# The feature-wise projections of a two-block language-model kernel: one 512-column matmul for the high weights, blocks of 256 features

## What is computed

```
zxbcdt = x @ w_in            # 2048 -> 10304: z, xs, B, C, dt
xbc = silu(conv4(xbc) + b);  y = chunked_scan(xs, dt, a, B, C) + xs * d
h = group_rms(y * silu(z)) * norm_w @ w_out;        x = layernorm(ALPHA * x + h)
k, v = x @ kv_w + kv_b;  q, gate = x @ w_bi         # window attention with sinks
x = layernorm(ALPHA * x + (attention(q, k, v) * silu(gate)) @ w_bo)
x = x + neighbourhood_attention(rms(x) @ w_qkv) @ w_o
x = x + relu(rms(x) @ w_1)**2 @ w_2                 # hidden size 8192
```

## Time and profile before

| | us |
|---|---|
| median of 3 runs | 2156.46 (2156.21 to 2156.93) |
| the profiled execution | 2156.41 |
| its span, first to last instruction | 2154.6 |
| PE busy in the span | 2138.8 (99%) |
| DVE busy | 1347.5 (63%) |
| ACT busy | 1124.4 (52%) |
| POOL busy | 18.4 |
| granted TensorE clock, mean | 1.000, so 2.4 GHz |

### The profile page before, as it was taken

The page is one execution under the profiler, slowest core; times in us unless marked ns, Lnnn a source line. Parts: engine busy times, 40 slices in busy tenths (PEclk is TensorE's granted clock), DMA queues, the critical chain, the costliest instruction groups (busy, mean ns, idle before and its releaser), DMA issues.

```text
span 2154.6 us, 33241 instructions
## 1 busy us (share of the span) xinstructions
PE 2138.8 (99%) x13589; PEld 1920.5 (89%) x13589; DVE 1347.5 (63%) x2126; ACT 1124.4 (52%) x1903; POOL 18.4 (1%) x30
## 2 busy tenths in 40 slices
PE   8999999999999999999999999999999999999999
PEld 8999999999887878998788888889998889999887
DVE  6877777777655887755855555555554445555443
ACT  5565666666444555643645666544444334444332
POOL 0000000000000000000000000000000000000000
PEclk9999999999999999999999999999999999999999
DMA  7555555555675543466565554455556665555664
GB/s 267 192 186 183 188 193 172 182 187 194 215 239 177 192 152 127 140 221 192 168 215 193 179 174 151 149 183 181 183 185 192 191 194 186 185 184 185 192 213 136
DMA packets 109640, 399.55 MB, mean 185 GB/s; under 512 B 12128, under 2 KB 12512, under 8 KB 108848
## 3 DMA queue, kind: packets, MB, share of 16 engines
q1 hardware_dynamic: 105552, 378.73, 54.4%
q0 software_dynamic: 3936, 18.70, 2.4%
HBM read 395.21 MB, written 2.16 MB: 184 GB/s over the span
## 4 chain that ended last, share of the span: by engine, by line
PE 97%; DVE 2%; ACT 1%; DMA 0%; issue 0%; SPq 0%; ACTq 0%; DVEq 0%
PE ps L1460 95%; PE ps L1463 2%; DVE wlo L862 1%; ACT lnt L556 0%; DMA raw<-in_w_in 0%; DVE xlo L862 0%; DVE small L868 0%; ACT xhi L559 0%; DVE res L871 0%; ACT whi L559 0%; DVE sms L865 0%; DVE sms L862 0%; DVE red L1270 0%; DVE qt L862 0%; DVE small L1120 0%
## 5 line engine op out<-in xcount | busy, mean ns | idle before, releaser
L862 DVE TENSOR_TENSOR wlo<-raw,whi 128x1024 fp32r<-128x1024 f32 (+1 forms) x713 | 869.9, 1223 | 664.5 <-ACT whi L559 662.9
L559 ACT ACTIVATE whi<-raw 128x1024 fp32r<-128x1024 f32 (+1 forms) x713 | 753.6, 1059 | 976.2 <-PE ps L1460 963.4
L1460 PE MATMUL ps<-xhi,whi 128*128 128x256 f32 x2560 | 728.7, 285 | 6.0 <-ACT whi L559 6.0
L1460 PE MATMUL ps<-xhi,wlo 128*128 128x256 f32 x2560 | 723.8, 283 | 0.7 <-DVE wlo L862 0.7
L1460 PE MATMUL ps<-xlo,whi 128*128 128x256 f32 x2560 | 723.7, 283 | 0.0
L1460 PEld LDWEIGHTS ps<-xhi,whi 128*128 128x128 f32 x2560 | 491.2, 192 | 10.4 <-issue 9.6
L1460 PEld LDWEIGHTS ps<-xhi,wlo 128*128 128x128 f32 x2560 | 491.1, 192 | 0.9 <-DVE wlo L862 0.9
L1460 PEld LDWEIGHTS ps<-xlo,whi 128*128 128x128 f32 x2560 | 491.3, 192 | 0.0
L1460 PE MATMUL ps<-whi,xhi 128*128 128x512 f32 x544 | 215.7, 402 | 3.1 <-ACT xhi L559 2.5
L1460 PE MATMUL ps<-whi,xlo 128*128 128x512 f32 x544 | 209.5, 392 | 0.1
L1460 PE MATMUL ps<-wlo,xhi 128*128 128x512 f32 x544 | 208.3, 390 | 0.0
(11 more groups left out here) (201 smaller groups left out, 1968.8 us busy)
## 6 DMA issues: line engine op xcount, KB each, us to landing
raw<-in_w SPq DMA_DIRECT2D x256, 512.0 KB, 3.5
raw<-in_w_in SPq DMA_DIRECT2D x159, 512.0 KB, 3.5
raw<-in_w_qkv SPq DMA_DIRECT2D x96, 512.0 KB, 3.5
raw<-in_w_ao SPq DMA_DIRECT2D x64, 512.0 KB, 4.3
raw<-in_w_bi SPq DMA_DIRECT2D x64, 512.0 KB, 3.5
raw<-in_w_bo SPq DMA_DIRECT2D x32, 512.0 KB, 4.4
raw<-in_w_o SPq DMA_DIRECT2D x32, 512.0 KB, 3.4
cum<-scratch POOLq DMA_DIRECT2D x8, 1024.0 KB, 5.9
```

The lines of the kernel that those rows point to most:

```text
L559: return eng.activation(out, x, ACT.Copy, **kw)
L862: return eng.tensor_tensor(out, x, y, op)
L1460: return eng.matmul(out, x, y, start=start, stop=stop, skip_group_check=True)
```

## The change

It has four parts, all in the feature-wise units.
- The two activation parts lie side by side (`xhl`: for each row 256 columns high, then 256 low). One matmul of 512 columns passes both through `whi` (called product 3), and one of 256 passes the high part through `wlo` (product 2). A block now fills a bank: columns 0 to 255 hold high x high, columns 256 to 511 the two others.
- So a unit is two blocks (256 features), and a slot four rows of 256 columns. There are 40 `in`, 8 `gate` and 32 `w1` units of four slots each. The number of slots, of visits and of bytes is unchanged.
- The halves are added at the end: ScalarE copies the second half of both banks to SBUF, VectorE adds the first half from PSUM onto it (`add_parts`). What follows (taps, tanh, silu, relu and square) reads the sum in SBUF. The banks come free when the sum is there, two visits after the unit's end at the earliest.
- The first two units of `in` and of each half of `w1` take turns slot by slot (`woven`), so that new rows of the activations are asked for as slowly as before.

```diff
-        self.tiles = nk // 2
+        self.rows = 4 if feat else 2
+        self.tiles = nk // self.rows
...
+    woven(features("in", 0, "w_in"), features("in", 1, "w_in"))
+    for n in range(2, 40):
+        slots.extend(features("in", n, "w_in"))
...
-            order = [(b, p) for p in range(3) for b in range(4)] if i == 0 else [(b, p) for b in range(4) for p in range(3)]
-            visits.append((i, None, [(i, 2 * j + h, b, p) for h in range(2) for b, p in order]))
+            order = [(b, p) for p in range(3) for b in range(2)] if i == 0 else [(b, p) for b in range(2) for p in (3, 2)]
+            visits.append((i, None, [(i, 4 * j + h, b, p) for h in range(4) for b, p in order]))
...
+            def copy_others(u, out):
+                w.wait_ge(S["weights"], END[u, 0])
+                w.wait_ge(S["weights"], END[u, 1])
+                return copy(out, main_and_rest(u)[1])
@@ in_proj on ScalarE @@
+                yield
+                w.wait_ge(S["conv"], convs_before[max(n - 1, 0)])
+                copy_others(INDEX["in", n], sums[:, n % 2, :, :]).then_inc(S["part"], 1)
+                yield 2
+                w.wait_ge(S["sum"], n + 1)
@@ in_proj on VectorE @@
+                yield 2
+                w.wait_ge(S["part"], n + 1)
+                add_parts(INDEX["in", n], sums[:, n % 2, :, :]).then_inc(S["sum"], 1)
                 yield 2
                 last = {}
                 for s in (1, 2, 3):
...
-                        i = stt(z[:, s:T], feature_bank(u, b)[:, 0:T - s], t[3 - s], ALU.mult, z[:, s:T], ALU.add)
+                        i = stt(z[:, s:T], sums[:, n % 2, b, 0:T - s], t[3 - s], ALU.mult, z[:, s:T], ALU.add)
...
-                    yield
-                yield
+                    if s == 1:
+                        yield
+                yield 2
@@ hidden on VectorE @@
+                add_parts(INDEX["w1", U], x.rearrange("p (k t) -> p k t", k=2)).then_inc(S["hsum"], 1)
+                w.wait_ge(S["hsum"], U + 1)
+                stt(x, x, 0.0, ALU.max, x, ALU.mult).then_inc(S["hsqr"], 1)
@@ wait_for_banks on TensorE @@
-                    w.wait_ge(S["tanh"], 4 * n + 4)
+                    w.wait_ge(S["sum"], n + 1)
...
+                    if p == 3:
+                        q = mul(bank, left, xhl[:, k, :, :].rearrange("p s t -> p (s t)"), start=k == 0, stop=False)
```

More of the change, by code:

```diff
@@ L72, in held_back, with woven, features @@
             slots.extend(part)
-    for n in range(20):
-        slots.extend(unit("in", n, "w_in", 8 * n, 16, feat=True))
+    def woven(a, b):
+        for pair in zip(a, b):
+            slots.extend(pair)
+    def features(stage, n, src):
+        return unit(stage, n, src, 4 * n, 16, feat=True)
+    woven(features("in", 0, "w_in"), features("in", 1, "w_in"))
+    for n in range(2, 40):
+        slots.extend(features("in", n, "w_in"))
     held_back(*[unit("ao", n, "w_ao", 16 * n, 32, apart="end" if n == 3 else None) for n in range(4)])
@@ L79, in plan @@
         slots.extend(unit("q", n, "w_bi", 8 * n, 16))
-    for n in range(4):
-        slots.extend(unit("gate", n, "w_bi", 32 + 8 * n, 16, feat=True))
+    for n in range(8):
+        slots.extend(features("gate", n, "w_gate"))
     held_back(*[unit("bo", n, "w_bo", 8 * n, 16, apart="end" if n == 3 else None) for n in range(4)])
@@ L89, in plan @@
     for half in range(2):
-        for n in range(8):
-            slots.extend(unit("w1", 8 * half + n, "w_1", 64 * half + 8 * n, 16, feat=True))
+        woven(features("w1", 16 * half, "w_1"), features("w1", 16 * half + 1, "w_1"))
+        for n in range(2, 16):
+            slots.extend(features("w1", 16 * half + n, "w_1"))
         held_back(*[unit("w2", 4 * half + n, "w_2", 64 * half + 16 * n, 32) for n in range(4)])
@@ L136, in marks @@
             last["used", i] = v, m
-            last["end", u, t // 2 if units[u].feat else t] = v, m
+            last["end", u, t] = v, m
     used, end, count, where = {}, {}, {}, {}
@@ L154, in feed @@
     sync, high, low = out[0]
-    for k in range(2):
-        for z in (sync, high, low):
-            z.extend([("x", k, 1), ("w", 0, k)])
+    for z in (sync, high, low):
+        z.extend([("x", 0, 1), ("w", 0, 0), ("x", 1, 1), ("x", 2, 2), ("w", 0, 1)])
     on = {"fetched": 1, "high": 1, "low": 1}
@@ L599, in in_proj @@
                     t, shift = taps(g, x)
-                    act(ACT.Identity, place(g, x), feature_bank(u, b), bias=shift, scale=t[3]).then_inc(S["ev"], 1)
-                yield 4
-                w.wait_ge(S["ssum"], sum(scan_at(g) + 18 < ended("in", n) + 5 for g in range(GROUPS)))
+                    act(ACT.Identity, place(g, x), sums[:, n % 2, b, :], bias=shift, scale=t[3]).then_inc(S["ev"], 1)
+                yield 3
                 for b, x in enumerate(blocks_of[n]):
-                    w.wait_ge(S["made"], 4 * (n - 1) + b + 1)
+                    w.wait_ge(S["made"], 2 * (n - 1) + b + 1)
                     if b in convs[n]:
@@ L713, in gates @@
             def gates(n):
-                u = INDEX["gate", n]
                 yield
                 w.wait_ge(S["roped"], 5)
[L717 to L727, removed]
+                w.wait_ge(S["g_low"], n - 1)
+                copy_others(INDEX["gate", n], gate[:, n % 2, 0, :].rearrange("p (k t) -> p k t", k=2)).then_inc(S["gpart"], 1)
+                yield 2
+                w.wait_ge(S["gsum"], n + 1)
+                act(ACT.Tanh, gate[:, n % 2, 1, :], gate[:, n % 2, 0, :], scale=0.5).then_inc(S["g_tanh"], 1)
+                yield 2
+                w.wait_ge(S["g_z"], n + 1)
+                copy(ghi[:, 2 * n:2 * n + 2, :], gate[:, n % 2, 0, :].rearrange("p (k t) -> p k t", k=2)).then_inc(S["g_high"], 1)
             def values(n):
@@ L1416, in vector_program @@
             side.at(19, rope_tables())
[L1417 removed]
+            for n in range(40):
                 side.at(ended("in", n), in_proj(n))
@@ L1531, in product @@
                 if unit.feat:
-                    right = factor(unit, k, (0, 1), p == 1)
-                    left = weight(i, k, p == 2)
-                    q = mul(feature_bank(u, x), left[:, x * P:x * P + P], right[:, k, :], start=k == 0 and x % 2 == 0 and p == 0, stop=last)
+                    left = weight(i, k, p == 2)[:, x * P:x * P + P]
+                    bank = ps[:, banks(u)[x], :]
+                    if p == 3:
+                        factor(unit, k, (0, 1), 0)
+                        factor(unit, k, (0, 1), 1)
+                        q = mul(bank, left, xhl[:, k, :, :].rearrange("p s t -> p (s t)"), start=k == 0, stop=False)
+                    else:
+                        right = factor(unit, k, (0, 1), p == 1)[:, k, :]
+                        q = mul(bank[:, 0:T] if p == 0 else bank[:, T:2 * T], left, right, start=k == 0 and p == 0, stop=last)
                 else:
```

157 lines of the change are left out of this document (75 added, 82 removed).

## The result

The changed kernel takes **2145.25 us** (median of 4 runs, 2144.99 to 2145.81) where the kernel before takes 2156.36 on the same chip: a ratio of 0.9948 with a 95% interval of [0.9931, 0.9966]. It is faster, by 11.1 us, but 8 us outside the range that was given and 16.7 us above the forecast.

A forecast was written before the change was run, and what follows sets the result against it. The prediction took PE's instruction stream to bound the kernel. From 2156.4 us it took 34.2 for the merge and added 5.3 (slot 16) and 1.1 (woven pairs): 2128.6 us, range 2122 to 2137.

The forecast's parts named there:

- What bounds the kernel: Whole kernel: PE's instruction stream sets the time, as long as the other engines stay ahead.
- The merge, -34.2 us: Feature-wise units: 2552 triples become a 512 and a 256, each saving 13.4 ns (360.0 to 346.6), all on the path.
- rival 3: Feature-wise units: the fixed part stays when widths alternate, a triple keeps 360.0 ns, 2162.8 us; chance 4%.
- Slot 16, +5.3 us: Near the start, PE waits for unit 2's addition, queued on DVE behind the time-step chain: +5.3 us.
- The woven pairs, +1.1 us: Units taking turns in `in` and each half of `w1`: PE waits 0.5 us and twice 0.3 us for additions.
- DVE and ACT at nothing: Steady stages: DVE's extra additions and ACT's extra copies hide behind PE's stream and cost nothing.
- Rivals 1 and 4: Small waits in many places, 2136 to 2143 us, 13%; the bank stall in every group, 2165.6 us, 5%.
- All but the merge: The stall at slot 16 and the waits of the woven pairs together: +6.4 us.

The follow-up runs named there:

- split: The changed kernel with the merge undone, so every matmul of the feature-wise groups has 256 columns: 2164.73 us, 1.0035 of the kernel before.
- add_first: The changed kernel with the in-projection steps, including the halves' addition, ahead of the time steps in DVE's side work: 2139.48 us, 0.9921 of the kernel before.
- kick: The changed kernel with order 512, 512, 256, 256 in the first 128 rows of each slot, alternating in the rest: 2139.24 us.
- lead_add: The changed kernel with the addition ahead of the time steps and runs of two in the first of each block's four slots: 2134.81 us.
- cross: The changed kernel, widths still alternating, but each 256 behind a 512 adds to the other bank than that 512: 2145.46 us.
- other_half: The changed kernel with the 256-column matmul adding to columns 0 to 255 of its bank instead of 256 to 511: 2145.28 us.

## Why the prediction was wrong

**What bounds the kernel**: right. PE 99% before and after, and the chain that ended last is 96% PE.

**The merge, -34.2 us**: this is the step that failed. It read: "I take 346.6, because the fixed part is equal at either width, so nothing in it seems to depend on the neighbour." That the fixed part is equal holds for uniform streams, before and after (120.0 ns in *split*, 226.6 in `w2`). The second half does not follow from it, and it is wrong: in strict alternation a triple took 353.3 ns in `w1` and in about two thirds of each `in` group, and 346.7 only in the rest (17% of all triples, counted by start times). *split* against the changed kernel puts the merge at 18.8 us, so the term was 15.4 us too large, most of the 16.7 us by which the forecast was too low. 353.3 lay within the bounds named in that step (320 to 360.0), but no rival stood for a part of the fixed cost: rival 3 kept all of it, with 4%, and the range left it out. Half of 34.2 lost would have given 2145.7. An unshown adjacency between two known rows should have kept its upper bound in the range.

The Trainium skill ("TensorE: Matmul & The Clock Gate", section "Back-to-back issue gap") gives N/2.4 + 2.5 ns for a matmul alone. For load and matmul pairs that is not what is seen here, neither uniform (120.0 ns for 256 columns in *split*, 226.6 for 512 in `w2`) nor mixed (353.3 or 346.7 for the two).

**Slot 16, +5.3 us**: the mechanism, the place and the wait were right (PE idle 5.21 us, from DVE's `sums` at 62.61 to 63.31 us; the forecast had it ready 16.4 us after PE went on with slot 12, and it was 63.31 - 46.89 = 16.4). Its price was not: the clock fell during the wait and slot 16 took 4.91 us, 2.1 more than at full clock. The prediction did not say a word on the clock. *add_first* supports the sum: it took away 5.21 + 2.1, put 0.63 of new waits in their place, and gained 5.8 us, 6.3 between the two traced executions, where this makes 6.7.

**The woven pairs, +1.1 us**: slot 8 waited 0.49 us for `sums` (0.5 forecast), and each half of `w1` has a wait of 0.24 (0.3 forecast). Place and idle time are right. By start times they cost more than they stand idle: from slot 7 to slot 9 are 6.37 us where two slots without a wait take 5.60, and each wait in `w1` costs 0.5 in the same way, so 1.8 in all.

```profile
PE ps L1476 <- DVE rl L878: 0.5, 2, 0.2
```

**DVE and ACT at nothing**: right. No wait of PE for either shows from 100 to 510 us. DVE's busy time rose to 1395.7 (near 1398 forecast), ACT's by 22.1 us (25 forecast). Rivals 1 and 4 did not occur.

**All but the merge** was forecast at +6.4 us. With the clock's 2.1 it is 8.5, and by start times 9.2 (7.4 at slot 16, 1.8 at the woven pairs). *split* measured 7.5 [4.7, 10.4].

**The sum again**: 2156.4 - 18.8 + 7.5 = 2145.1, measured 2145.25. The two parts are both taken from *split*, so this sum is no test of its own. The trace alone gives one: -17.0 (2552 x 6.67) - 3.0 (some 450 triples in the quick rhythm, 6.67 more each) + 7.4 (slot 16: from the last matmul of slot 15 at 57.87 to the one behind slot 16 at 68.20 are 10.33 us, where some 2.95 would do without stall and slow clock) + 1.8 (the three other waits) makes 2145.6. The traced execution took 2145.81.

**What stays open**: why TensorE loses 20 ns in three triples in one rhythm and nothing in the other, and what about an interruption selects it. That a turned row always switches the rhythm in *kick* is seen, not explained, and neither *lead_add* nor the waits follow so simple a rule. The runs exclude the bank, the half of the bank, the merged matmul by itself and a fixed price per change of width. The number of changes matters in no simple way (1 in 1: 0 or 6.7 ns a triple; runs of two 1.7; of four 3.3 to 4.2; of eight 2.5).

## What to carry to other kernels

A saving that rests on "so many matmuls fewer" is safe only for streams that the trace shows. Where two widths are going to stand side by side for the first time, keep the full fixed cost as an end of the range, and try several orders of the same matmuls: here a one-line change of order was worth almost as much as the whole edit (9.5 against 11.1 us). When an edit makes TensorE wait on a vector engine's side work, first see whether that side work can be put in another order, and price a wait of some microseconds with the slow work behind it (1.7 to 2.7 us here).

## What the runs showed of the hardware that was not expected

- One and the same sequence of loads and matmuls has two paces at the same granted clock of 1.00: 346.7 and 353.3 ns for a 512 and a 256. Each lasts over a hundred microseconds (868 against 851 matmuls in 150 us in *cross*), and it changed behind a wait of 0.24 us in *cross*, while the same wait in the changed kernel left it. In *kick* one row of another order switched it each time, 267 times of 267.
- Runs of two (512, 512, 256, 256) have one pace in every stage looked at, 348.3 ns a triple, and beat both longer runs and what strict alternation comes to.
- The granted clock fell to 0.50 (1.2 GHz) during a wait of 5.2 us and stayed there for the first 4.1 us of the work behind it; in *other_half* for 3.2 and in *cross* for 5.4, behind a wait of the same length. By the Trainium skill, "TensorE: Matmul & The Clock Gate", section "Part 1: The HAM clock gate", an idle array falls to half rate and has to be active to get its full rate back; the rows at 60 to 68 us agree with both.
